# Values and gates of one recurrence projected inside the scan of another, and eight diagonal products in one bank

## The reference

```
proj = rmsnorm(h) @ w_in        # split into q_sb.. z_ssd x b c dt | q_hg f_hg i_hg g_hg

# SSD, per chunk (a = dt * -exp(A_log)):
acum   = cumsum(a);  decay = masked exp(acum_t - acum_s)
y_diag = ((C B^T) * decay) @ (x * dt)
y_off  = (C @ state) * exp(acum)
state  = state * exp(acum_end) + B^T @ (exp(acum_end - acum) * x * dt)
y      = (y_diag + y_off + x * d_skip) * silu(z)

# HGRN2: the same kind of scan, with q = silu(q_hg), k and log f from f_hg,
#        values v = i_hg, and at the end
o      = rmsnorm(o) * silu(g_hg)
```

## Time and profile before

| | |
|---|---|
| median of three runs | 4328.2 us |
| the profiled execution | 4332.95 us |
| its span in the profile | 4331.1 us |
| TensorE busy over the span | 3929.7 us (91%) |
| VectorE busy | 2012.0 us (46%) |
| ScalarE busy | 1288.6 us (30%) |
| GpSimd busy | 697.6 us (16%) |

### The profile page before, as it was taken

How to read it: one execution, slowest core, us unless ns; L and a number is a source line. 1 busy time by engine, 2 the same in 40 slices (tenths; PEclk the granted TensorE clock), 3 DMA queues, 4 the chain that set the end, 5 groups by cost and what they waited for, 6 DMA issues and landing times. The chain is left out here.

```text
span 4331.1 us, 50822 instructions
## 1 busy us (share of the span) xinstructions
PE 3929.7 (91%) x19548; PEld 2409.5 (56%) x19548; DVE 2012.0 (46%) x3920; ACT 1288.6 (30%) x2390; POOL 697.6 (16%) x868
## 2 busy tenths in 40 slices
PE   6999988899998999789989897896988999999998
PEld 3655556655545554566554454555457468537843
DVE  3477445433534575554253304426135444565465
ACT  3245234423412443353252115422611311001100
POOL 2300320010005002201100102204022100340033
PEclk8999999999999999999999999998999999999999
DMA  4101330001011011000012110000000122443243
GB/s 168 44 18 37 121 128 1 1 32 48 28 68 54 32 37 54 30 1 1 35 46 80 59 48 1 1 25 15 20 20 4 63 100 84 149 181 111 79 174 146
DMA packets 108175, 253.80 MB, mean 59 GB/s; under 512 B 5200, under 2 KB 33872, under 8 KB 107552
## 3 DMA queue, kind: packets, MB, share of 16 engines
q1 hardware_dynamic: 102288, 231.86, 15.1%
q10 hardware_dynamic: 4384, 12.58, 0.8%
q0 software_dynamic: 1264, 6.11, 0.3%
HBM read 223.27 MB, written 27.26 MB: 58 GB/s over the span
## 5 line engine op out<-in xcount | busy, mean ns | idle before, releaser
L667 PE MATMUL ps<-ring,hT 128*128 128x384 f32 (+3 forms) x2208 | 692.6, 471 | 16.8 <-PEq L268 6.1
L667 PEld LDWEIGHTS ps<-ring,hT 128*128 128x128 f32 x2208 | 396.0, 195 | 273.6 <-issue 144.5
L1079 DVE TENSOR_REDUCE stat_a<-ps 128x1 f32<-128x1280 f32 (+1 forms) x144 | 196.6, 1368 | 181.2 <-PE ps L938 181.2
L977 PE MATMUL ps<-hT,ring 128*128 128x512 f32 (+1 forms) x640 | 280.2, 551 | 0.0
L1340 PE MATMUL ps<-ring,YT 128*128 128x512 f32 x576 | 250.2, 592 | 1.3 <-PEq L1136 1.3
L1019 ACT ACTIVATE YT<-ps,stat_a 128x1280 f32<-128x1280 f32 (+1 forms) x144 | 177.5, 1233 | 199.6 <-DVE stat_a L1079 197.7
L1262 DVE TENSOR_REDUCE stat_b<-ps 128x1 f32<-128x1280 f32 (+1 forms) x108 | 143.2, 1367 | 128.7 <-PE ps L1153 128.7
L1704 ACT ACTIVATE hid<-hid 128x1024 f32<-128x1024 f32 x32 | 33.8, 1057 | 550.0 <-DVE hid L1784 550.0
L1724 POOL TENSOR_TENSOR Wd<-ring 128x512 f32<-128x512 f32 x64 | 85.1, 1330 | 680.5 <-DMA ring<-in_w_down 598.8
L1682 PE MATMUL ps<-Wd,const 128*128 128x512 f32 x384 | 186.8, 595 | 0.1
L1340 PEld LDWEIGHTS ps<-ring,YT 128*128 128x128 f32 x576 | 108.1, 190 | 131.4 <-issue 131.4
(11 more groups left out here) (441 smaller groups left out, 6928.7 us busy)
## 6 DMA issues: line engine op xcount, KB each, us to landing
ring<-in_w_down SPq DMA_DIRECT2D x32, 2048.0 KB, 7.9
ring<-in_w_up SPq DMA_DIRECT2D x16, 2048.0 KB, 7.8
ring<-in_w_in SPq DMA_DIRECT2D x14, 2048.0 KB, 7.7
adaw_b<-in_w_ada SPq DMA_DIRECT2D x16, 1024.0 KB, 5.3
ring<-in_w_out SPq DMA_DIRECT2D x6, 2048.0 KB, 8.2
ring<-in_w_in SPq DMA_DIRECT2D x6, 1536.0 KB, 6.6
x<-res SPq DMA_DIRECT2D x18, 512.0 KB, 2.9
gates<-const SPq DMA_DIRECT2D x32, 256.0 KB, 2.1
```

Of the source, the lines that this page charges most:

```text
L667: mm = pe.matmul(ps[:, n % 2, 0:hi - lo], hT[:, k, t * P:(t + 1) * P], w[:, k, lo:hi], start=(k == 0), stop=(k == KC - 1))
L977: mm = pe.matmul(ps[:, GB, 0:hi - lo], pr.view(i0 + c)[:, k, b % 4 * P:(b % 4 + 1) * P], hT[:, k, lo:hi], start=(k == 0), stop=(k == KC - 1))
L1079: dve.tensor_reduce(st[:, i % 4, m:m + 1], scored_at(i, m), AX, ALU.max, negate=True)\
```

## The change

The second weight piece of the gated recurrence (values and gates, H_I) changes places with the first (H_Q), so that it is in the ring when `stage_ssd` begins. `stage_ssd` takes over its nine units: 0, 1 and 2 whole, around the decay sums and in chunk 0; each other one in two halves, over the chunks 1 to 6, one half behind the transposes and one before the diagonal products. They accumulate in bank 2 (unit 1 in bank 5). ScalarE copies values and raw gates out of it, and takes the Silu over all gates once at the end of the stage. C·B moves from bank 2 to the upper half of bank 1 and waits for ScalarE's copies of the transposes. The eight diagonal products go side by side into bank 6, 64 columns apart; each but the last still writes 128 columns, of which the next one overwrites the upper half. VectorE then adds them in one instruction, and B's transposes wait for `W_ready` of the last chunk in place of `y_out`. `stage_hg_project` keeps nine units, and its last transposes stand at the end of the stage. The values reuse the buffer of the stick-breaking stage's values, whose tail columns are already set, so a memset on GpSimd goes.

```diff
--- stage_ssd
@@ setup
+    VB, FREE = 2, {1: 5}
+    LEADS = 3
+    def dense_at(i):
+        u = LEADS + i - 1
+        return u if i >= 1 and u < L2T else None
+        @block.sync
+            pr.load_more(sp, 1)
@@ ScalarE
+            def keep_values(u):
+                act.wait_ge(*S["proj_done"](u + 1))
+                bank = FREE.get(u, VB)
+                ins = act.activation(Vh[:, u, 0:HW], ps[:, bank, 0:HW], ACT.Copy)
+                if u:
+                    ins = act.activation(Y[:, u - 1, 3 * HW:4 * HW], ps[:, bank, HW:2 * HW], ACT.Copy)
+                ins.then_inc(*S["v_used"].inc())
...
             act.activation(sc[:, 0, :], sc[:, 0, :], ACT.Ln, bias=1.0).then_inc(*S["log1p"].inc())
+            keep_values(0)
             act.wait_ge(*S["decay_sums"](1))
             act.activation(E[:], ps[:, 0, 0:3 * NH].rearrange("p (a n) -> p a n", a=3), ACT.Exp).then_inc(*S["decays"].inc())
+            keep_values(1)
             for i in range(L2T):
...
+                if i == 0:
+                    keep_values(2)
...
+                if dense_at(i) is not None:
+                    keep_values(dense_at(i))
+            act.wait_ge(*S["v_used"](L2T))
+            act.activation(Y[:, :, 3 * HW:4 * HW], Y[:, :, 3 * HW:4 * HW], ACT.Silu)
@@ VectorE
+            dve.tensor_tensor(dt[:], dt[:], spread(dtb, [P, L2T, H], 1), ALU.add).then_inc(*S["dt_biased"].inc())
             dve.memset(xdt[:, H * HD:], 0.0)
             dve.memset(st[:], 0.0).then_inc(*S["state_zero"].inc())
-            dve.tensor_tensor(dt[:], dt[:], spread(dtb, [P, L2T, H], 1), ALU.add).then_inc(*S["dt_biased"].inc())
...
-                    step(dve.tensor_tensor(cbm[:], ps[:, 2, 0:2 * P].rearrange("p (g n) -> p g n", g=2),
+                    step(dve.tensor_tensor(cbm[:], ps[:, 1, 2 * P:4 * P].rearrange("p (g n) -> p g n", g=2),
...
-                    for g, bank in enumerate((6, 1)):
-                        tg = heads(t1[:])[:, 4 * g:4 * g + 4, :]
-                        ins = dve.tensor_tensor(tg, tg, ps[:, bank, :].rearrange("p (h d) -> p h d", h=4)[:, :, 0:HD], ALU.add)
-                    step(ins)
+                    step(dve.tensor_tensor(t1[:], t1[:], ps[:, 6, :], ALU.add))
@@ TensorE
+            def dense(u, ks):
+                if u >= LEADS:
+                    pe.wait_ge(*S["v_used"](u))
+                elif u == 2:
+                    pe.wait_ge(*S["v_used"](1))
+                for k in ks:
+                    mm = pe.matmul(ps[:, FREE.get(u, VB), :], hT[:, k, u * P:(u + 1) * P], w[:, k, :], start=(k == 0), stop=(k == KC - 1))
+                if ks[-1] == KC - 1:
+                    mm.then_inc(*S["proj_done"].inc())
+            def part(i, ks):
+                if dense_at(i) is not None:
+                    dense(dense_at(i), ks)
+            pr.arrived(pe, i0)
+            dense(0, every)
             pe.wait_ge(*S["a_ready"](1))
...
             mm.then_inc(*S["decay_sums"].inc())
+            dense(1, every)
             pe.wait_ge(*S["decays"](1))
...
                 if i >= 2:
-                    pe.wait_ge(*S["y_out"](i - 1))
+                    pe.wait_ge(*S["W_ready"](i - 1))
                 for b in range(2):
                     mm = pe.transpose(ps[:, 1, b * P:(b + 1) * P], convT[:, 4 + b, ch], c["ident"])
                 mm.then_inc(*S["turned"].inc())
+                if i == 0:
+                    dense(2, every)
+                part(i, [0, 1, 2, 3])
                 if i >= 1:
-                    if i >= 2:
-                        pe.wait_ge(*S["W_ready"](i - 1))
+                    pe.wait_ge(*S["xB_kept"](i + 1))
                     for g in range(2):
-                        mm = pe.matmul(ps[:, 2, g * P:(g + 1) * P], convT[:, 4 + g, ch], convT[:, 6 + g, ch], start=True, stop=True)
+                        mm = pe.matmul(ps[:, 1, (2 + g) * P:(3 + g) * P], convT[:, 4 + g, ch], convT[:, 6 + g, ch], start=True, stop=True)
...
                     pe.wait_ge(*S["state_new"](i))
+                    if i == 1:
+                        pe.wait_ge(*S["v_used"](2))
...
                     mm.then_inc(*S["state_sum"].inc())
+                part(i, [4, 5, 6, 7])
                 if i >= 1:
                     pe.wait_ge(*S["W_ready"](i))
...
                     for h in range(H):
-                        at = (h % 4) * P
-                        mm = pe.matmul(ps[:, (6, 1)[h // 4], at:at + WIDE], W[:, h, :], xdt[:, h * HD:h * HD + WIDE],
-                                       start=True, stop=True)
+                        wide = WIDE if h + 1 < H else HD
+                        mm = pe.matmul(ps[:, 6, h * HD:h * HD + wide], W[:, h, :], xdt[:, h * HD:h * HD + wide],
+                                       start=True, stop=True, skip_group_check=True)
+            pe.wait_ge(*S["proj_done"](L2T))
+            pe.sem_inc(pr.spent, 1)
--- stage_hg_project
-            pr.load_more(sp, 2)
+            pr.load_more(sp, 1)
...
+            for t in range(n):
+                if t >= 2:
+                    pe.wait_ge(*S["f_used"](t - 1))
...
+                if t >= LAG:
+                    turn(t - LAG)
+            pe.wait_ge(*S["proj_done"](n))
+            pe.sem_inc(pr.spent, 1)
+            for t in range(n - LAG, n):
+                turn(t)
...
-            for t in range(n):
-                act.wait_ge(*S["proj_done"](n + t + 1))
-                b = (n + t) % 2
-                ins = act.activation(Vh[:, t, 0:W], ps[:, b, 0:W], ACT.Copy)
-                if t:
-                    ins = act.activation(Y[:, t - 1, 3 * W:4 * W], ps[:, b, W:2 * W], ACT.Silu)
-                ins.then_inc(*S["v_used"].inc())
-                if t == 0:
-                    keep(n - 1)
-            pool.memset(Vh[:, :, W:], 0.0)
+            keep(n - 1)
--- plan_weights
+    add(w, (H_I, 3336))
     add(w, (H_Q, H_I))
-    add(w, (H_I, 3336))
```

More of the change, by code:

```diff
@@ L2050, in stage_conv, with stage_ssd @@
     pr.end(2)
-def stage_ssd(pr, convT, Y, dt, par, c, b_):
+def stage_ssd(pr, hT, convT, Vh, Y, dt, par, c, b_):
     nc, S, ps = pr.nc, pr.S, pr.ps
+    i0 = pr.next_use
     H, NH = SSDH, L2T * SSDH
@@ L2061, in stage_ssd, with _ @@
     GW = SSDH // SSDG * HD
+    HW = HGH * HD
+    VB, FREE = 2, {1: 5}
+    LEADS = 3
     def heads(ap):
         return ap.rearrange("p (h d) -> p h d", d=HD)
+    def dense_at(i):
+        u = LEADS + i - 1
+        return u if i >= 1 and u < L2T else None
     with nc.Block() as block:
+        @block.sync
+        def _(sp):
+            pr.load_more(sp, 1)
         @block.scalar
@@ L2164, in _ @@
         def _(pe):
+            w = pr.view(i0)
+            def dense(u, ks):
[10 more added lines that the diff above has]
+                    dense(dense_at(i), ks)
+            every = list(range(KC))
+            pr.arrived(pe, i0)
+            dense(0, every)
             pe.wait_ge(*S["a_ready"](1))
@@ L2211, in _, with stage_hg_project @@
                     for h in range(H):
-                        at = (h % 4) * P
-                        mm = pe.matmul(ps[:, (6, 1)[h // 4], at:at + WIDE], W[:, h, :], xdt[:, h * HD:h * HD + WIDE],
-                                       start=True, stop=True)
+                        wide = WIDE if h + 1 < H else HD
+                        mm = pe.matmul(ps[:, 6, h * HD:h * HD + wide], W[:, h, :], xdt[:, h * HD:h * HD + wide],
+                                       start=True, stop=True, skip_group_check=True)
                     mm.then_inc(*S["diag_done"].inc())
-    pr.end()
-def stage_hg_project(pr, hT, qk, Kt, LF, Vh, Y, c, work):
+            pe.wait_ge(*S["proj_done"](L2T))
+            pe.sem_inc(pr.spent, 1)
+    pr.end(1)
+def stage_hg_project(pr, hT, qk, Kt, LF, c, work):
     nc, S, ps = pr.nc, pr.S, pr.ps
@@ L2242, in turn @@
                 mm.then_inc(*S["qkT_ready"].inc())
[L2244 to L2250, removed]
+            pr.arrived(pe, i0)
+            w = pr.view(i0)
+            for t in range(n):
+                if t >= 2:
+                    pe.wait_ge(*S["f_used"](t - 1))
                 for k in range(KC):
-                    mm = pe.matmul(ps[:, u % 2, :], hT[:, k, t * P:(t + 1) * P], w[:, k, :], start=(k == 0), stop=(k == KC - 1))
+                    mm = pe.matmul(ps[:, t % 2, :], hT[:, k, t * P:(t + 1) * P], w[:, k, :], start=(k == 0), stop=(k == KC - 1))
                 mm.then_inc(*S["proj_done"].inc())
[L2254 to L2258, removed]
+                if t >= LAG:
[4 more added lines that the diff above has]
+                turn(t)
         @block.scalar
@@ L2316, in _ @@
                 dve.tensor_copy(rot[:, t % 2, W:2 * W], Kt[:, t, :]).then_inc(*S["k_ready"].inc())
-    pr.end(2)
+    pr.end(1)
 def stage_hg(pr, qk, Kt, LF, Vh, OH, c, b_):
@@ L2737, in build @@
             every = list(range(L2T))
-            with nc.sbuf_tensor("qk_sb", [P, 4, L2T * P], F32) as qk, nc.sbuf_tensor("v_sb", [P, L2T, SBH * HD + WIDE - HD], F32) as V:
```

(6 more changed lines are left out.)

6 lines of the change are left out of this document (2 added, 4 removed).

## The result

The changed kernel takes 4297.43 us (median of four runs, 4294.11 to 4304.07) against 4328.11 (four runs) for the one before: a ratio of 0.9930, 95% interval 0.9913 to 0.9947. That is 30.7 us less; 29.8 were forecast. The profiled execution took 4298.45 us, with a span of 4296.6.

What follows compares the result with a forecast made beforehand. The chain between engines bounds the scan, TensorE's rate the projection's second half. Projection -54.7, scan +21.9, stage behind +3.0 make -29.8: 4328.2 to 4298.4 us, range 4291 to 4314.

Steps and rivals of the forecast that it cites:

- The chunk: Scan, chunks 1 to 6: 6.6 us of own products plus a 6.9 us unit, 13.5 us each if TensorE never waits.
- The covers: Scan, chunks 1 to 6: TensorE work in front of each dependence exceeds the other engines' time, so TensorE never waits.
- Chunk 7: Scan chunk without a unit: waits of 1.1 us for the copies and 1.1 before the diagonal products, 8.8 us in all.
- The first unit: Unit 0 at the scan's start: 6.9 us plus 1.7 for 3.4 us at 1.2 GHz, to 2936.9.
- One bank for eight products: Scan's diagonal products, each overwriting half of the last: taken as 0, between bounds of nothing and 19 us.
- The stage behind: Next scan after projection: TensorE arrives from near idleness, first sums at half clock; +3 us, between +1.7 and +8.
- (A): Scan gaps stay partly open: clock stays at 0.84 (4314) or the shared bank slows diagonal products (4317); chance 0.17.
- (B): A covered wait falls one to two us short in each full chunk: +6 to +12, about 4307; chance 0.15.
- (C): Slower: units push back the scan's chain from segments to Y; less than 12 of 36 idle us filled; +12, 4340; chance 0.05.
- (D): No gain: freed time returns in the stage behind, its clock staying low, 25 us in all; within 0.2%; chance 0.03.
- The 12.3 us before the decay sums: TensorE's wait before the scan's first sums, counted in the 36 idle us and used as an argument against (C).
- the price that I put on a failed cover: Scan: if a cover failed, it would cost the present wait, 2.75 us in every chunk.

Runs made afterwards that it cites:

- kernel 1: Kernel before with the bank changes and their waits alone, all eighteen units left in the projection stage: 4309.26 us, 0.9958.
- Kernel 4: Changed kernel with all eight diagonal products 64 columns wide, so that none overwrites another's columns: 4306.12 us, 0.9944.
- (5): The changed kernel run once more, unedited, to measure the spread: 4299.58 us, 0.9931 of the kernel before.
- kernels 3: Kernel 2 plus three surplus matmuls of 512 columns, result unread, before the wait for Y in each of seven chunks: 4317.87 us, 0.9974.
- 6: Changed kernel plus one surplus unit, result unread, in front of the projection stage's uncovered last transposes: 4295.26 us, 0.9924.
- Kernel 7: Changed kernel with unit 0 moved into the idle tail of the convolution stage, unit 1 taking its place: 4288.65 us, 0.9908.
- Kernel 2: Changed kernel with B's transposes again waiting for the last chunk's finished Y, units kept in the scan: 4328.0 us, 1.0000.

## Why the prediction was right

**The sum.** Forecast -54.7 + 21.9 + 3.0 = -29.8. Between the two profiled executions: projection stage -53.2, scan +21.3, next scan +1.0. The stage that was expected to lose its pure half lost it, and what came back in the scan was well under half of it: TensorE's idle time there fell by 27.9 us, and its busy time rose by only 49.2 for nine units worth 62.0, since the scan's clock went from 0.84 to 0.97.

**The chunk** was told at 13.5 us and took 13.22. The diagonal products take 1.73, not 1.89, two transposes 0.22, not 0.27, and four 0.44, not 0.5. The 1.89 and the 0.27 are distances between starts, as the prediction says, but the earlier trace rows has both behind a wait, and a row behind a wait takes longer: in the changed kernel's chunk 7, where the diagonal products are waited for again, they take 1.84. Six chunks are 1.7 us less than told.

**The covers.** Each was told to be larger than what it covers. All hold: there is no wait in chunks 1 to 6. **Chunk 7** was told at 8.8 and took 9.06; its two waits alone, in a kernel without units (1), gave 8.69.

**The first unit** was told at 8.6 us and took 9.95 from start to start (9.34 in the second execution). This was the largest miss of a single piece of work: I took the price of a cold start from the row behind a pause of 3.3 us, and this pause was 7.8. That +1.4 and the -1.7 of the chunks are what makes the scan look exact (21.3 against 21.9): two misses that cancel, which is luck.

**One bank for eight products** was taken at nothing between ends of 0 and 19 us. Kernel 4 leaves the overlap out and its products take the same 1.73 us. Behind a wait the one bank takes 1.84 us, the two banks of the kernel before 1.89. To take nothing for it was right.

**The stage behind.** 82.0 us were told, 83.5 came: +0.45 from the last transposes, as told, and +1.3 from a longer cold start than the earlier trace rows show. That is no property of the change: the same program took 80.5 us when the clock did not fall there (5). The next scan's first sums were told near 4 us and took 4.18 and 3.83; of the +3.0 for that stage one profile shows +1.0, the other +3.4. The Trainium skill (TensorE: Matmul & The Clock Gate, The HAM clock gate) makes the slow clock the default that activity lifts; kernels 3, 6 and 7 agree, each by making TensorE busy ahead of the slow piece (5.29 to 3.60, 4.18 to 2.18, 10.11 to 7.11 us).

**The rivals.** (A) needed 0.84 for the clock in the scan; it is 0.97. (B) needed a wait in each full chunk; there is none. (C) needed less than 12 of 36 idle us to go; 28 went, 9.5 of them by the banks alone (26.5 us are left idle in kernel 1). (D) needed 25 us back in the stages behind; 1.0 to 3.4 came.

**What was wrong though the sum did not hang on it.** The 12.3 us before the decay sums were counted among the 36 idle us of the scan, and (C) was argued against with them. Only 4.5 of them lie in it; the other 7.8 are the pause in front of unit 0, which the sum has in its place. Kernel 7 is the one that fills it. The second error is the price that I put on a failed cover, "2.75 us in every chunk". Kernel 2 makes exactly that cover fail: 2.6 us of wait, and then up to 1.7 us more because the next half unit runs at half clock. The total is 29.2 us in the scan, where seven waits alone are 18.1. With that price in the sum, (C) would have had a mechanism: the same nine units in the scan, in the new banks but with the wait for Y left in, bring nothing at all (1.0000). The two halves of the change are not additive. The banks with the wait removed give 17.7 us; the units moved with the wait kept give 0; all together give some 30.

**Open:** why the same pause costs nothing in one execution and 3.0 us in the next; that activity lifts the clock does not say it. The single executions of the changed kernel and its variants differ by several us, and the pauses between stages that show such a choice account for a part of it; no run was made that sets it.

## What to carry to other kernels

Before filling an engine's gaps with another stage's work, remove the waits that make the gaps, by a buffer or a bank; work put beside a remaining wait keeps the wait and may run at half clock behind it. Then cut the moved work so that each dependence is covered by just enough of it, and spread it over all the gaps, those at stage ends included: banks and units together gave 30 us with the nine units in the changed kernel's places, and 55 when the stage ends were used too and the rest spread evenly. Read the rate of work that will not wait from a row that does not wait, and a cold start's price at a pause of the same length.

## What the runs showed of the hardware

- A pause of 2.6 us in front of a busy stretch was followed by half clock in some places of one execution and not in others (5.29 and 3.60 us for the same eight records). One of 3.3 us, at the start of the projection stage, cost nothing in four of eleven executions and 1.4 to 3.1 us in the other seven. One of 7.8 us, at the start of the scan, cost 2.4 to 3.0 us in each of the seven executions where a unit follows it.
- Surplus matmuls can make a kernel faster: 21 of them, each 0.86 us of TensorE's time, took 10 us off kernel 2.
- A MATMUL record of these float32 products takes 0.108 us at 64 columns as at 128 (1.73 us for 16 from start to start, in kernel 4 and in the changed kernel).
